# A GLA/SSD/conv-FFN decoder layer: the first four gate pairs of the up projection as plain products of unnormalised h

## The chip, the cores and the metric

The kernel runs on one core of one Trainium2 chip. The metric is the time of one execution in device microseconds. Engines are named as in the profile: PE multiplies matrices, DVE, ACT and POOL work elementwise, SP issues DMAs.

## The reference

One layer on 576 tokens: 512 of one new sequence and 64 of eight running ones (8 each). D_MODEL is 2048, FFN_DIM 5632, all in fp32.

```python
def _layer(x, s_gla, s_ssd, s_conv, s_ffn, p):
    xn = _rmsnorm(x, p['n_mix_pre'])
    mix, g_new, h_new, c_new = _mixer(xn, s_gla, s_ssd, s_conv, p)
    x = x + _rmsnorm(mix, p['n_mix_post'])          # h
    xn = _rmsnorm(x, p['n_ffn_pre'])
    f, f_new = _conv_ffn(xn, s_ffn, p)
    x = x + _rmsnorm(f, p['n_ffn_post'])
    return x, g_new, h_new, c_new, f_new

def _conv_ffn(xn, s_ffn, p):
    u = xn @ p['ffn_w_in']                          # 2048 -> 2 x 5632
    u, buf = _causal_dwconv(u, s_ffn, p['ffn_conv_w'], p['ffn_conv_b'])
    a, b = jnp.split(u, 2, axis=-1)
    return (jax.nn.silu(a) * b) @ p['ffn_w_out'], buf.astype(xn.dtype)
```

## The kernel before

Activations lie transposed: 128 features on the partitions, 576 tokens (T) along the free axis, HALF = 288 of them in a PSUM bank. A vector of 2048 features is KT = 16 k tiles. Each fp32 product is made of three fast ones (type fp32r): both factors are split into a high part, rounded by ACT's copy, and a low part, the rest, subtracted by DVE or POOL; then hi x hi, hi x lo and lo x hi are summed. Weights arrive in units of eight 128x128 blocks (512 KB): SP loads them into one of two `raw` slots, ACT writes w_hi (`weight_hi`, `two_hi`), POOL writes w_lo (`weight_lo`), in a ring of four. SP may refill a raw slot when its low part is done.

In order of time the kernel has the input projection with the GLA and SSD mixers woven in, the output projection (32 half tiles, until some 934 us), the h stage, the up projection with conv and gate, the down projection, and the last norm.

**The h stage.** While the output projection's second half runs, DVE adds its halves to the mix tiles, ACT squares them, and DVE adds the squares to `sqsum`. PE sums that over the partitions with one-column matmuls, ACT and DVE make the reciprocal root of the few columns, and PE spreads it over the partitions into PSUM (`work[:, 2:4]`). Then, tile by tile, DVE multiplies the mix tile by it and by norm_mix_post (semaphore h_m), POOL (tiles 0 to 10, POOL_H) or DVE (11 to 15) adds x: this is h. ACT squares h into one of two sq buffers and stores h to DRAM in pairs; PE's `h_arrives` sums the square of a tile over the partitions with six one-column matmuls and adds three fill-in matmuls (`keep_clock` does so elsewhere). When all 16 are summed, the root is made again, spread by PE and copied to `rstd`.

**The up projection.** It makes 2 x 44 tiles of 128 features: 44 pairs (FT) of a gate tile and its partner. Each pair is computed by Winograd's form of the 2x2 product: the two output tiles by two halves of the k tiles, against two halves of the tokens. Seven products take the place of eight. For each pair of k tiles j (KP = 8), DVE's `form(j)` normalises h (two multiplies) and makes four sums and differences (T1 to T4); with the three plain parts these are seven operands of 288 columns. ACT's `x_highs(j)` copies all 2016 columns, DVE's `x_lows(j)` subtracts 1440 of them and POOL's `x_lows(j)` 576. A unit of weights serves two k pairs: 14 products of three matmuls; DVE forms four sums from it (`weight_sums`), ACT rounds both (`hi_a`, `hi_s`), DVE subtracts both (`weight_lows`). A pair has four units, so 4 x 2 x 7 x 3 = 168 matmuls of 288 columns. Its seven products sit in seven of eight banks; ACT's `p1_copy` reads the first, DVE's `evacuate(g)` the others. The conv's taps (`tap_zero` on ACT, `taps_of` on DVE), `silu` on ACT, `gate_product` on DVE and `g_out` (ACT stores the result) of a pair run during the next one. Each engine's order is the order of its program, written out in loops over w, the weight units.

**The down projection** reads the stored products back, splits them (`g_high`, `g_low`) and multiplies chunk by chunk of k.

## Time and profile before

| | us |
|---|---|
| median of three runs | 2622.26 |
| the runs | 2621.03 to 2623.07 |
| profiled execution, its own time | 2619.91 |
| its span, first to last instruction | 2618.1 |

| busy | us | share of the span |
|---|---|---|
| PE | 2543.0 | 97% |
| DVE | 1616.5 | 62% |
| ACT | 929.8 | 36% |
| POOL | 598.8 | 23% |

Times in the trace count from the start of the span. The page cuts the span into 40 slices; PE's busy share is 90% or more in all but a few: two of them, at some 980 to 1110 us, have 6 and 8 tenths, and the granted clock falls there to 7 and 6 tenths. A busy PE isn't PE at its peak: ends of matmuls are modelled, so the distance from start to start tells the pace. The view by stretches gives each engine's busy time and the granted clock (1.00 is 2.4 GHz, 0.50 is 1.2 GHz). A number in brackets in the timeline is idle time ahead of the instruction, with what ended it.

### The profile page before, as it was taken

The page shows a single profiled execution, that of the slowest core. Times are in us where ns is not written, and L with a number is a line of the kernel's source. Part 1 is how long each engine was busy: PE and PEld are TensorE (multiplying, and loading weights), DVE is VectorE, ACT ScalarE, POOL GpSimd, SP SyncE. Part 2 cuts the span into 40 slices and gives each one's busy share as a digit, 9 for nine tenths or more (in the row PEclk, how much of TensorE's full clock was granted, in tenths as well). Part 3 has the DMA queues.
Part 4 walks back from the last instruction along what each step waited for, and adds up shares of the span by engine and source line. Part 5 has one row for each costly group of instructions (what it writes and reads, how often), then busy time and mean ns, then how long its engine had stood idle before and what let it go on. Part 6 is the DMA issues. An engine that isn't in the chain of part 4 may idle for free.

```text
span 2618.1 us, 49296 instructions
## 1 busy us (share of the span) xinstructions
PE 2543.0 (97%) x20790; PEld 2513.7 (96%) x20790; DVE 1616.5 (62%) x2335; ACT 929.8 (36%) x1288; POOL 598.8 (23%) x285
## 2 busy tenths in 40 slices
PE   8999999999999996899999999999999999999996
PEld 7999999999999996899999999999999999999996
DVE  6544555764336346999999999999999311212105
ACT  6332222533232223544444444444445222112112
POOL 3333223433133321000000000000001334333337
PEclk9999999999999976999999999999999999999998
DMA  4222238523554211333333333333335423242422
GB/s 176 88 83 85 81 123 274 189 74 91 184 187 151 81 63 35 104 111 111 111 104 110 108 107 106 110 111 110 105 110 160 148 88 126 81 134 90 153 84 86
DMA packets 96823, 303.31 MB, mean 116 GB/s; under 512 B 10080, under 2 KB 14816, under 8 KB 95600
## 3 DMA queue, kind: packets, MB, share of 16 engines
q1 hardware_dynamic: 58336, 211.84, 26.4%
...
q14 instruction: 46, 0.38, 0.0%
...
## 4 chain that ended last, share of the span: by engine, by line
PE 88%; DVE 7%; DMA 2%; ACT 1%; POOL 1%; issue 1%; ACTq 0%; POOLq 0%; DVEq 0%; SPq 0%
PE psum_proj L1172 17%; PE psum_proj L1627 9%; PE psum_proj L1628 9%; PE psum_proj L1629 9%; PE psum_work L1627 9%; PE psum_work L1628 9%; PE psum_work L1629 9%; PE psum_proj L1174 8%; PE psum_work L1607 1%; PE psum_work L1612 1%; POOL arena L540 1%; DVE ops_a L2347 1%; DVE arena L2180 1%; DMA out_ssd_s_dram<-arena 1%; DMA raw<-in_weights_dram 1%
## 5 line engine op out<-in xcount | busy, mean ns | idle before, releaser
L483 POOL TENSOR_TENSOR w_lo<-raw,w_hi 128x1024 fp32r<-128x1024 f32 x210 | 521.0, 2482 | 1893.8 <-ACT w_hi L1035 1295.6
L1172 PE MATMUL psum_proj<-x_hi,w_hi 128*128 128x288 f32 (+2 forms) x1696 | 510.6, 301 | 15.0 <-DVE x_lo L1761 13.0
L1172 PE MATMUL psum_proj<-x_lo,w_hi 128*128 128x288 f32 (+2 forms) x1696 | 501.4, 296 | 0.0
L1174 PE MATMUL psum_proj<-x_hi,w_lo 128*128 128x288 f32 (+2 forms) x1696 | 500.8, 295 | 0.0
L1172 PEld LDWEIGHTS psum_proj<-x_hi,w_hi 128*128 128x128 f32 x1696 | 320.6, 189 | 22.2 <-issue 15.5
L1172 PEld LDWEIGHTS psum_proj<-x_lo,w_hi 128*128 128x128 f32 x1696 | 319.8, 189 | 2.6 <-issue 1.9
L1174 PEld LDWEIGHTS psum_proj<-x_hi,w_lo 128*128 128x128 f32 x1696 | 319.5, 188 | 0.0
L550 ACT ACTIVATE w_hi<-raw 128x1024 fp32r<-128x1024 f32 x122 | 128.8, 1056 | 463.1 <-PE psum_proj L1174 402.7
L1627 PE MATMUL psum_proj<-ops_a,w_hi 128*128 128x288 f32 x934 | 276.7, 296 | 6.9 <-DVE ops_a L2290 6.7
L1627 PE MATMUL psum_work<-ops_a,w_hi 128*128 128x288 f32 x916 | 272.4, 297 | 5.4 <-DVE ops_a L2347 5.1
L1628 PE MATMUL psum_proj<-ops_a,w_hi 128*128 128x288 f32 x934 | 276.1, 296 | 0.0
L1629 PE MATMUL psum_proj<-ops_a,w_lo 128*128 128x288 f32 x934 | 276.1, 296 | 0.0
L1629 PE MATMUL psum_work<-ops_a,w_lo 128*128 128x288 f32 x916 | 271.5, 296 | 0.0
L1628 PE MATMUL psum_work<-ops_a,w_hi 128*128 128x288 f32 x916 | 271.4, 296 | 0.0
L1035 ACT ACTIVATE w_hi<-raw 128x1024 fp32r<-128x1024 f32 x88 | 93.3, 1060 | 421.1 <-PE psum_proj L1629 215.4
L907 ACT ACTIVATE w_hi<-tail 128x1024 fp32r<-128x1024 f32 x117 | 124.3, 1063 | 219.1 <-DVE tail L2230 219.1
L1627 PE MATMUL psum_proj<-ops_b,w_hi 128*128 128x288 f32 x608 | 180.4, 297 | 6.7 <-DVE ops_b L2290 6.7
L1627 PEld LDWEIGHTS psum_proj<-ops_a,w_hi 128*128 128x128 f32 x934 | 176.4, 189 | 7.6 <-issue 6.9
L1627 PEld LDWEIGHTS psum_work<-ops_a,w_hi 128*128 128x128 f32 x916 | 173.5, 189 | 7.3 <-DVE ops_a L2347 3.9
L1628 PE MATMUL psum_proj<-ops_b,w_hi 128*128 128x288 f32 x608 | 180.0, 296 | 0.0
L1629 PE MATMUL psum_proj<-ops_b,w_lo 128*128 128x288 f32 x608 | 179.8, 296 | 0.0
L1628 PEld LDWEIGHTS psum_proj<-ops_a,w_hi 128*128 128x128 f32 x934 | 176.3, 189 | 0.0
...
## 6 DMA issues: line engine op xcount, KB each, us to landing
raw<-in_weights_dram SPq DMA_DIRECT2D x386, 512.0 KB, 3.6
...
```

Of the source, the lines that this page charges most:

```text
L483: nc.gpsimd.tensor_tensor(w_lo[:, slot], raw[:, r], w_hi[:, slot].bitcast(F32), ALU.subtract).then_inc(lo_ready, 1)
L540: nc.gpsimd.tensor_tensor(a, a, cut(x_hi[:, kt].bitcast(F32), n), ALU.add).then_inc(added_p, 1)
L550: nc.scalar.activation(w_hi[:, slot], raw[:, r], ACT.Copy).then_inc(hi_ready, 1)
L907: nc.scalar.activation(w_slot(w, 0)[:, 6:14], w_sum, ACT.Copy).then_inc(whs_ready, 1)
L1035: nc.scalar.activation(w_hi[:, (2 + v) % 4], raw[:, v % 2], ACT.Copy).then_inc(hi_ready, 1)
L1172: nc.tensor.matmul(banks[:, n, 0:b - a], w_hi[:, slot, k], (hi, lo)[part][:, a:b], start=first and part == 0, stop=False)
L1174: mm = nc.tensor.matmul(banks[:, n, 0:b - a], w_lo[:, slot, k], hi[:, a:b], start=False, stop=last)
L1607: mm = nc.tensor.matmul(work[0:w, 0, 448 + 3 * n + i:449 + 3 * n + i], cut(sq[kt % 2], n)[:, t:t + w], ones[:, 0:1], start=kt == 0 and n = ...
L1612: nc.tensor.matmul(work[:, 1, 0:P], ones[:], ident[:], start=True, stop=True)
L1627: nc.tensor.matmul(to, w_h, hi, start=first, stop=False)
L1628: nc.tensor.matmul(to, w_h, lo, start=False, stop=False)
L1629: return nc.tensor.matmul(to, w_l, hi, start=False, stop=last)
```

## The change

The first four gate pairs (STD = 4) are no longer computed by seven products but by the eight of the plain form, 2 outputs x 16 k tiles x 2 cuts of the tokens x 3 matmuls, from operands that aren't normalised yet: ACT writes h x norm_ffn_pre as the high part as each h tile comes (`x_std`), DVE the low part (`x_low_std`). The factor 1/rms of a token is applied when DVE reads the banks (`take_std`). So PE can start with the first h tile; in the first pair each k tile's square is summed over the partitions by two matmuls of 288 columns against a full matrix of ones (`sum_tokens`), which leaves the sum on all partitions; ACT's root and DVE's reciprocal then run on all 576 columns. The six one-column matmuls, the fill-in matmuls of a tile, the spreading of the root by PE and the copy of it go.

The operands of the seven products are formed during the plain pairs: DVE normalises h in place behind the first pair, and `form`, `x_highs` and `x_lows` come in pieces as room is freed. The plain operands of the 16 k tiles take the room of the seven-product operands, so pairs 2 to 5 of these wait for the fourth plain pair's progress (`tile_mm`, STD_FREES) and are written out by hand in the programs of ACT and DVE. POOL now adds x for all 16 tiles, splits the weights of the 16 plain units as it does in the projections before, and no longer takes a part of the x low parts. The x rows are reloaded into other room, earlier, right behind the last GLA part. The seven-product form runs over 40 pairs. The last pair takes its units in the order 1, 2, 0, 3, the down projection its banks in another order, and h comes back with its tiles swapped in pairs, all as the layout asks.

The core of the diff:

```diff
+STD = 4
+W_UNIT0 = FFN_UNIT0 + STD * UP_UNITS
+WUNITS = (FT - STD) * UP_UNITS
...
+STD_FREES = (1, 5, 10, 12)
+LAST_UNITS = (1, 2, 0, 3)
...
+        def x_std(kt, low):
+            if kt < 2:
+                return w_third[:, T * (2 * kt + low):T * (2 * kt + low + 1)]
+            slot = 2 * kt - 4 if kt < 6 else 2 * kt + 4 if kt < 12 else 2 * kt - 16
+            return ops_a[:, T * (slot + low):T * (slot + low + 1)]
...
-            for kt in range(POOL_H):
+            weights_lo(at_ynorm + 1, at_h - 1)
+            for j in range(4):
+                if j == 3:
+                    pool.wait_ge(sq_free, KT + 2)
+                weight_lo(4 * at_h - 2 + j, (2 + j) % 4, j % 2)
+            for kt in range(KT):
                 pool.wait_ge(h_m, kt + 1)
-                pool.wait_ge(block_in[kt // 4], 16)
+                pool.wait_ge(block_in[kt // 4], 64 if kt >= 12 else 16)
                 nc.gpsimd.tensor_tensor(h_of(kt), h_of(kt), xres(kt), ALU.add).then_inc(added_p, 1)
-            x_lows(0)
-            x_lows(1)
...
+            weights_lo(at_h, (W_UNIT0 - 2) // 4)
...
+                    two_hi(4 * i + OUT_UNIT0 + 4 + d0, 2 * i + OUT_UNIT0 // 2 + 2 + d0 // 2, 2)
+                    for j in range(4):
+                        act.wait_ge(taken, 4 * i + j + OUT_TILE0 + d0 + 3)
+                        act.wait_ge(sq_free, 4 * i + j + 8 * c + 1)
+                        nc.scalar.activation(sq[j % 2], mix_of(c, i, j).rearrange("p o t -> p (o t)"),
+                                             ACT.Square).then_inc(squared, 1)
+                        if j == 1:
+                            two_hi(4 * i + OUT_UNIT0 + 6 + d0, 2 * i + OUT_UNIT0 // 2 + 3 + d0 // 2, 0)
...
+                act.wait_ge(added_p, kt + 1)
+                nc.scalar.activation(x_std(kt, 0), h_of(kt), ACT.Copy, scale=V("ffn_pre", kt)).then_inc(op_high, 1)
                 if kt >= 2:
                     act.wait_ge(hsq_mm, kt - 1)
                 nc.scalar.activation(sq[kt % 2], h_of(kt), ACT.Square).then_inc(squared, 1)
...
+                if kt == 11:
+                    hi_std(4)
...
             act.wait_ge(hsq_mm, KT)
-            roots_of_columns(work[:, 0, 448:451], work[:, 0, 451:454], mroot)
-            hi_a(1)
-            act.wait_ge(msum_mm, 3)
-            nc.scalar.activation(halves(rstd[:]), work[:, 0:2, 0:HALF], ACT.Copy).then_inc(mroot, 1)
+            root(rstd[:], work[:, 0:2, 0:HALF], 1.0 / D, mroot)
+            hi_std(5)
...
+                a = DIRECT * HALF
+                nc.scalar.activation(x_ops(j, 0)[:, 0:a], h_pair(j)[:, 0:a], ACT.Copy)
+                nc.scalar.activation(x_ops(j, 0)[:, a:], x_sums(j)[:, a:], ACT.Copy).then_inc(op_high, 1)
...
+            hi_std(6)
+            hi_std(7)
+            states_in(0)
+            tap_zero(0, 0)
+            tap_zero(0, 1)
+            new_states(0)
+            silu(0)
+            g_out(0)
+            hi_std(8)
+            hi_std(9)
             x_highs(0)
             x_highs(1)
+            hi_std(10)
+            hi_std(11)
+            states_in(1)
+            tap_zero(1, 0)
+            tap_zero(1, 1)
+            new_states(1)
+            silu(1)
+            g_out(1)
+            hi_std(12)
+            hi_std(13)
+            hi_std(14)
+            hi_std(15)
+            hi_a(0)
+            states_in(2)
+            tap_zero(2, 0)
+            tap_zero(2, 1)
+            hi_s(0)
+            new_states(2)
+            silu(2)
+            g_out(2)
+            x_highs(2)
+            hi_a(1)
             hi_s(1)
-            for w in range(WUNITS):
-                g, u = w // UP_UNITS, w % UP_UNITS
+            x_highs(3)
+            x_highs(4)
+            hi_a(2)
+            x_highs(5)
+            hi_s(2)
+            states_in(3)
+            tap_zero(3, 0)
+            tap_zero(3, 1)
+            act.wait_ge(taken, UP_TAKEN0)
+            act.dma_start(fstate[:, 672:], fconv_in.rearrange("p b c -> p (b c)")[:, 672:]).then_inc(ffn_in, 16)
+            x_highs(6)
+            x_highs(7)
+            hi_a(3)
+            hi_s(3)
+            new_states(3)
+            hi_a(4)
+            hi_s(4)
+            silu(3)
+            g_out(3)
...
+                sum_tokens([sq[kt % 2]], 0, hsq_mm, kt == 0, kt == KT - 1)
+                pe.wait_ge(op_low, kt + 1)
+            def up_std(g):
+                order = LAST_STD if g == STD - 1 else range(KT)
+                steps = [(0, 1, 2, 3)] + [(i,) for i in range(4, KT)] if g == 1 else [(i,) for i in range(KT)]
+                rings = (3, 2) if g % 2 else (1, 0)
+                if g >= 2:
+                    pe.wait_ge(taken, STD_TAKEN0 + 2 * (g - 1))
+                for step in steps:
+                    for j in range(2):
+                        if g == 1 and j and 0 in step:
+                            pe.wait_ge(mroot, 2)
+                        for i in step:
+                            kt = order[i]
+                            half, k = kt // 8, kt % 8
+                            n = 4 * g + 2 * half + j
+                            if g == 0 and j == 0:
+                                h_arrives(kt)
+                            if i % 8 == 0:
+                                pe.wait_ge(lo_ready, FFN_UNIT0 + n + 1)
+                            mm = products((2 + n) % 4, k, rings[j], 256, i == 0, i == KT - 1, x_std(kt, 0), x_std(kt, 1))
+                            if j and i % 8 == 7:
+                                mm.then_inc(units_done, 2)
+                            if j and g == STD - 1 and i in STD_FREES:
+                                mm.then_inc(tile_mm, 1)
+            for g in range(STD):
+                up_std(g)
...
+                    if g == STD:
+                        pe.wait_ge(op_low, X_OPS0 + kp + 1)
...
+                            if g == STD and q in (0, 4):
+                                pe.wait_ge(taken, UP_TAKEN0 - (2 if q == 0 else 0))
...
+            def x_low_std(kt):
+                ve.wait_ge(op_high, kt + 1)
+                stt(x_std(kt, 1), h_of(kt), V("ffn_pre", kt), x_std(kt, 0).bitcast(F32), ALU.mult, ALU.subtract)\
+                    .then_inc(op_low, 1)
...
+                if kt >= 2:
+                    x_low_std(kt - 2)
...
+            ve.wait_ge(mroot, 2)
+            own(nc.vector.reciprocal(rstd[:], rstd[:]))
+            settle()
+            def normalise(j):
+                h = h_pair(j)
+                stt(h[:, 0:T], h[:, 0:T], V("ffn_pre", 2 * j + 1), rstd[:], ALU.mult, ALU.mult)
+                own(stt(h[:, T:2 * T], h[:, T:2 * T], V("ffn_pre", 2 * j), rstd[:], ALU.mult, ALU.mult))
...
+                if 2 <= j < 5:
+                    ve.wait_ge(tile_mm, j)
+                if j == 5:
+                    ve.wait_ge(units_done, W_UNIT0)
+                if j in (1, 6, 7):
+                    ve.wait_ge(op_low, X_OPS0 + j)
...
+                tt_op(x_ops(j, 1)[:, 0:a], h_pair(j)[:, 0:a], x_ops(j, 0)[:, 0:a].bitcast(F32), ALU.subtract)
+                tt_op(x_ops(j, 1)[:, a:], x_sums(j)[:, a:], x_ops(j, 0)[:, a:].bitcast(F32), ALU.subtract)\
...
+            def take_std(g, j):
+                pd, banks = fpad[j], pair_of_banks(((1, 0), (3, 2))[g % 2][j])
...
+                tt_op(pd[:, FC - 1:FC - 1 + SEQ].rearrange("p (n t) -> p n t", n=2), banks[:, :, 0:256],
+                      rstd[:, 0:SEQ].rearrange("p (n t) -> p n t", n=2), ALU.mult)
+                tt_op(sample_cols(pd[:, FC - 1 + SEQ:])[:, :, FC - 1:], sample_cols(banks[:, 1, 256:320]),
+                      sample_cols(rstd[:, SEQ:T]), ALU.mult).then_inc(taken, 1)
...
+            take_std(0, 0)
+            take_std(0, 1)
+            ve.wait_ge(h_st, 128)
+            for j in range(4):
+                normalise(j)
+            taps_of(0, 0)
+            taps_of(0, 1)
+            for j in range(4, KP):
+                normalise(j)
+            gate_product(0)
+            for j in range(2):
+                form(j)
+                x_lows(j)
+            take_std(1, 0)
+            take_std(1, 1)
+            taps_of(1, 0)
+            taps_of(1, 1)
+            gate_product(1)
+            take_std(2, 0)
+            take_std(2, 1)
+            weight_sums(0)
+            taps_of(2, 0)
+            taps_of(2, 1)
+            weight_lows(0)
+            gate_product(2)
+            form(2)
             weight_sums(1)
-            x_lows(0)
-            x_lows(1)
-            for w in range(WUNITS):
-                g, u = w // UP_UNITS, w % UP_UNITS
-                if g == 0 and u < 3:
-                    form(2 * w + 2)
+            x_lows(2)
+            weight_lows(1)
+            form(3)
+            form(4)
+            x_lows(3)
+            x_lows(4)
+            take_std(3, 0)
+            take_std(3, 1)
+            form(5)
+            weight_sums(2)
+            x_lows(5)
+            weight_lows(2)
+            weight_sums(3)
+            form(6)
+            x_lows(6)
+            form(7)
+            x_lows(7)
+            weight_lows(3)
+            weight_sums(4)
+            taps_of(3, 0)
+            taps_of(3, 1)
+            gate_product(3)
```

## Rows read from the trace of the kernel before

**Rows 1.** The page, busy time, share of the span and instructions: PE.
```profile
PE 2543.0 (97%) x20790; PEld 2513.7 (96%) x20790; DVE 1616.5 (62%) x2335; ACT 929.8 (36%) x1288; POOL 598.8 (23%) x285
```
**Rows 2.** Stretches: length, busy us of each engine (instructions), PE clock, DMA share, GB/s.
```profile
942.00:950.00 8.00, 8.00 (x73) 7.85 (x72) 8.00 (x13) 2.73 (x4) 7.82 (x6) 1.00 0.51 174
950.00:970.00 20.00, 20.00 (x106) 19.66 (x105) 10.10 (x11) 4.10 (x6) 8.80 (x6) 0.52 0.27 101
...
1012.00:1027.00 15.00, 7.69 (x44) 7.52 (x45) 14.83 (x19) 4.59 (x4) 3.97 (x3) 0.73 0.12 36
...
1400.00:1800.00 400.00, 400.00 (x3026) 400.00 (x3025) 378.56 (x631) 191.32 (x289) 0.00 (x0) 1.00 0.36 109
```
**Rows 3.** Timeline of ACT (start, duration, what): the copies of a first product.
```profile
1061.72 0.41 ACT L972 ACTIVATE smalls<-psum_proj 128x288 f32<-128x288 f32 x1 [0.56 <-PE psum_proj L1629]
...
1085.17 0.41 ACT L972 ACTIVATE smalls<-psum_work 128x288 f32<-128x288 f32 x1 [0.24 <-PE psum_work L1629]
...
2020.86 0.38 ACT L972 ACTIVATE smalls<-psum_work 128x288 f32<-128x288 f32 x1
```
**Rows 4.** Timeline of PE in the h stage and at the first seven-product matmul.
```profile
944.85 1.34 PE L1607 MATMUL psum_work<-ones,arena 128*128 128x1 f32 x12
...
954.88 2.18 PE L1607 MATMUL psum_work<-ones,arena 128*128 128x1 f32 x12
...
958.43 2.19 PE L1607 MATMUL psum_work<-ones,arena 128*128 128x1 f32 x12
...
1012.57 0.58 PE L1627 MATMUL psum_proj<-ops_a,w_third 128*128 128x288 f32 x1 [6.73 <-DVE ops_a L2290]
```
**Rows 5.** Timeline of PE at the kernel's start: sums of squares among projection matmuls.
```profile
28.23 1.13 PE L1204 MATMUL psum_work<-arena,ones 128*128 128x288 f32 x4
...
32.36 1.13 PE L1204 MATMUL psum_work<-arena,ones 128*128 128x288 f32 x4
```
**Rows 6.** Timeline of DVE: the post-norm multiplies of 16 tiles.
```profile
941.28 11.69 DVE L2256 SCALAR_TENSOR_TENSOR arena<-x_flat,vec,psum_work 128x576 f32<-128x576 f32 x16 [0.25 <-PE psum_work L1596]
```
**Rows 7.** Timeline of POOL: the adds of x, 11 tiles.
```profile
942.18 16.62 POOL L517 TENSOR_TENSOR arena<-arena,x_flat 128x576 f32<-128x576 f32 x11 [30.19 <-DVE arena L2256]
```
**Rows 8.** Timeline of DVE: first and last difference of a form, an x low part.
```profile
1003.15 0.46 DVE L2278 TENSOR_TENSOR x_flat<-x_flat 128x288 f32<-128x288 f32 x1
...
1004.39 0.45 DVE L2283 TENSOR_TENSOR x_flat<-x_flat 128x288 f32<-128x288 f32 x1
...
1024.53 1.65 DVE L2290 TENSOR_TENSOR ops_a<-x_flat,ops_a 128x1440 fp32r<-128x1440 f32 x1
```
**Rows 9.** Timeline of DVE: weight sums, taps, weight low parts, the next sums (first instructions).
```profile
1069.82 0.69 DVE L2226 TENSOR_TENSOR tail<-raw 128x512 f32<-128x512 f32 x1
...
1071.35 0.83 DVE L2332 SCALAR_TENSOR_TENSOR x_flat<-x_flat 128x592 f32<-128x592 f32 x1
...
1072.97 0.95 DVE L2235 TENSOR_TENSOR w_third<-raw,w_third 128x768 fp32r<-128x768 f32 x1
...
1075.16 0.69 DVE L2226 TENSOR_TENSOR tail<-raw 128x512 f32<-128x512 f32 x1
```
**Rows 10.** Timeline of DVE at the kernel's start: a reciprocal of all tokens.
```profile
42.55 3.75 DVE L1775 RECIPROCAL rstd<-rstd 128x576 f32<-128x576 f32 x1 [2.27 <-ACT rstd L562]
```
**Rows 11.** Timeline of DVE: one subtraction beside POOL's weight splits, and alone.
```profile
2016.59 15.70 DVE L2347 TENSOR_TENSOR ops_a<-x_flat,ops_a 128x576 fp32r<-128x576 f32 x11 [2.58 <-ACT ops_a L1028]
...
2057.22 0.75 DVE L2347 TENSOR_TENSOR ops_a<-x_flat,ops_a 128x576 fp32r<-128x576 f32 x1
```
**Rows 12.** Timeline of ACT: the high parts of one k pair's seven operands.
```profile
1004.88 1.88 ACT L965 ACTIVATE ops_a<-x_flat 128x2016 fp32r<-128x2016 f32 x1 [3.34 <-DVE x_flat L2283]
```
**Rows 13.** The page, DMA issues: KB each and median us to landing.
```profile
raw<-in_weights_dram SPq DMA_DIRECT2D x386, 512.0 KB, 3.6
```
**Rows 14.** The page, costliest groups: POOL's splits and ACT's copies of a weight unit.
```profile
L483 POOL TENSOR_TENSOR w_lo<-raw,w_hi 128x1024 fp32r<-128x1024 f32 x210 | 521.0, 2482 | 1893.8 <-ACT w_hi L1035 1295.6
...
L550 ACT ACTIVATE w_hi<-raw 128x1024 fp32r<-128x1024 f32 x122 | 128.8, 1056 | 463.1 <-PE psum_proj L1174 402.7
```

354 lines of the change are left out of this document (152 added, 202 removed).

## The prediction

> **What bounds the kernel now.** I read the page first: PE is busy 97% of the span [rows 1], so a change gains only where PE idles, runs at its lower clock, or is given less to do. The table of stretches names the place. In 1400 to 1800 us PE is busy throughout at clock 1.00, with DVE at 378.56 of 400 us; from 950 to 970 us PE looks busy at clock 0.52 (the stretch up to 1001 is like it), and from 1012 to 1027 it is busy for half of the time (the next two stretches of 15 us are like it) [rows 2]. The timeline of PE tells what it did: up to 997 us it summed squares with one-column matmuls and filled up with matmuls that nobody reads, one h tile in 3.55 us (954.88 to 958.43) [rows 4]. Then it waited for DVE four times, some 7 us each, because the operands of the seven products come in pairs from DVE (the wait of 6.73 before 1012.57 stands for the four). ACT's copy of the first product of each gate pair is a good clock hand: call its start S(g). S(0) = 1061.72, S(1) = 1085.17, S(43) = 2020.86 [rows 3]. From S(1) on a pair takes (2020.86 - 1085.17)/42 = 22.28 us, which is 168 matmuls at 0.1326 us. PE bounds that part, DVE is 5% behind it.
>
> So between the first h tile at 944.85 [rows 4] and S(0) lie 116.9 us for 150 matmuls (19.9 us) of useful work: 97 us are lost. The change lets PE multiply there. Everything up to some 934 us and everything from S(5) on is the same work in the same order (the order of the last pair's units and of the banks in the down projection only rename what is free), so the sum is the shift of S(5). Before, S(5) = 1085.17 + 4 x 22.28 = 1174.3.
>
> **Start.** ACT now makes the high part of the fourth plain unit ahead of the squares of the last two mixer tiles, and this copy waits for the last mixer matmul. It costs one copy of 1.06 us [rows 14], of which I take 0.75 as exposed (at most 1.1, at least 0: the last mixer tile has to be read by DVE first, and that runs beside it). DVE's first weight sum and split leave this place, but PE's fill-in matmuls covered them: nothing. The x tiles are loaded earlier, and nobody waits for them. First h sum on PE: 944.85 + 0.75 = 945.6.
>
> **First plain pair.** 16 k tiles x 2 outputs x 2 halves x 3 = 192 matmuls; at 0.1326 that is 25.5 us. The squares now go through 128x288 fp32 matmuls against ones. The trace has this pattern at its start: 24 projection matmuls with one such sum repeat every 32.36 - 28.23 = 4.13 us [rows 5], so a sum costs 4.13 - 24 x 0.1326 = 0.95 us, 16 of them 15.2. Is PE fed? It needs a tile every 2.54 us. POOL adds 16 tiles instead of 11 at 16.62/11 = 1.51 us [rows 7]; DVE gives 0.73 us to the post-norm [rows 6] and 0.75 to 1.5 us to the low part; ACT gives two passes, each at most as long as DVE's. All are quicker: PE bounds. The pair ends at 945.6 + 40.7 = 986.3. PE has dense work from 945.6 on, while its clock fell only at some 950 us, after 5 us of one-column matmuls [rows 2]; I take the full clock.
>
> The sum of a tile is its four instructions of 288 columns. The Trainium skill, FP8 and Floating Point Precision, lists true FP32 as four passes through the array; by that two matmuls would cost 8 x 0.133 = 1.06 us and the sixteen 17 us. The row, 0.95, is a little cheaper than this estimate, and I use the row.
>
> **Second pair.** It runs 25.5 us, to 1011.8. Its second output needs the bank of the sums and the next weight unit: root, weight copy and POOL split are 0.7 (an estimate from the 0.73 of DVE for as many columns) + 1.06 + 2.48 [rows 14] = 4.2 us against 1.6 + 3.2 us of PE work; covered, up to 0.5 if not. DVE starts at 985.5 with the reciprocal of 576 columns, 3.75 us [rows 10] (the old way inverted a few columns), then takes the first pair out (four multiplies from PSUM, 1.5, as the post-norm's 0.73 for 576 columns [rows 6]), then 4 pairs of normalisation, 8 x 0.74 = 5.9, taps 3.25 [rows 9], the other 8 normalisations 5.9, gate product 0.75. That is 1006.5 if DVE is alone. It isn't: POOL now splits twelve more units, and DVE's subtractions that cost 0.75 us alone took 15.70/11 = 1.43 while four POOL splits ran [rows 11], 1.9 us lost for each. Two splits fall into the normalisations: 1009.9. Behind that gate product ACT stands in g_out, and behind it the copies of units 8 and 9, which PE needs at once for the third pair: they end at 1011.0 and 1012.0, POOL's splits at 1013.5 and 1016.0. PE waits 1.7 and, after one step of 0.8, 1.7 more: 3.4 us (0 if DVE is undisturbed, 7 if each split costs its whole 2.48 and the normalisations queue). I add 1 for matmuls at the lower clock behind it; behind a wait of 6.7 us the trace has a dozen or more of them.
>
> The Trainium skill says this of the two engines (GPSIMD Engine Reference, Key points): GpSimd shares its SBUF interfaces with VectorE, and instructions with two SBUF inputs contend. [rows 11] agree, 1.43 against 0.75. It speaks against leaving the weight splits of the plain units to POOL.
>
> **Third and fourth pair.** Third: to 1011.8 + 3.4 + 1 + 25.5 = 1041.7. In it DVE has 29 us of work at most and reaches its end idle. Fourth: to 1067.2. Its work for DVE can't begin at 1041.7: the two weight buffers are held by units 14 and 15, whose copies wait for the third pair's end. Copy 1.06, split 2.48, DMA 3.6 [rows 13] put the first seven-product unit into place at 1048.8. From there DVE has, in its order: sums 1.53, a wait for ACT's first tap 0.4, taps 3.25, low parts 2.0 to 2.19, gate product 0.75, form 1.65, sums 1.5, wait 0.5, x low parts 2.3, weight low parts 2.1, two forms 3.3, x low parts 2.4 and 2.3: 24 us [rows 8, 9]. (A form is now only its four subtractions, 1003.15 to 1004.84; the x low parts cover 2016 columns where 1440 took 1.65 [rows 8], so 2.3, because POOL's share has gone to DVE.) Only then come the two reads of the fourth pair's banks, 1.5: 1074.3. But PE's fifth product of the fifth pair wants those banks at 1067.2 + 12 x 0.1326 = 1068.8. **First new wait: 5.5 us.**
>
> **Fifth pair.** From 1074.3 PE runs the ten products that are left of unit 0 (4.0, to 1078.3), unit 1 to 1083.9 and unit 2 to 1089.4. Unit 3 needs x pairs 6 and 7 and the fourth split of weights. DVE by then: three forms 5.0, two weight sums 3.0, three x low parts 6.8, two weight low parts 4.1, and between form and low part ACT's copy of 2016 columns, 1.88 [rows 12], exposed twice in full and once by 0.5 because this form, copy, subtract goes pair by pair: 4.4. Sum 23.3: 1097.6. **Second new wait: 8.2 us.** Before, POOL took 576 of the 2016 columns and two forms overlapped the copies.
>
> Then sums 1.5, taps 3.25, gate product 0.75, low parts 2.1: 1105.2, where PE has ended the pair at 1103.2; sums 1.5, and the pair's five bank reads at 0.46 us and a short wait each [rows 8] until PE's seventh product may start: 1109.6. From there to the first product of the last k pair are 132 matmuls, 17.5 us: S(5) = 1127.1. The clock behind the two waits hides under DVE; I add 0.5. 1127.6 against 1174.3 is **46.7 us** less. From here DVE has 1 us per pair in hand and PE's pitch of 22.28 holds.
>
> Check of the sum from the other side: 96 more matmuls (4 x 24) 12.7, sums 15.2, start 0.75, waits 3.4 + 1 + 5.5 + 8.2 + about 3.5 from S(4) to S(5) (4.7 there, less the 1.2 that S(0) to S(1) lost before) make 50.3; 97 less 50.3 is 46.7.
>
> The profiled execution took 2619.91 us for a span of 2618.1; it is 2.35 below the median of the three runs, 2622.26. 2619.9 - 46.7 = 2573.2, and at the median 2575.6: **2576 us**.
>
> **The rivals.**
> - *All waits are covered.* If DVE is little disturbed, the banks free earlier and the last operands come in time, PE alone bounds: 945.6 + 40.7 + 76.5 + 22.3 + 19.9 = 1105.0 for S(5), 69.3 less, **2553 us**. Against it stands DVE's share of 95% in the steady part [rows 2]: it has no room for the eight operand pairs, and the order take after form is fixed. Chance 0.10.
> - *DVE and ACT queue longer.* If each POOL split costs DVE 2.5 us, if a blocked wait of ACT (g_out, the weight copies behind it) repeats at the third and fourth pair, and if the sixth pair's backlog lasts, some 14 us come on top: **2590 us** (2585 to 2600). Chance 0.20.
> - *PE isn't fed in the first pair.* Now POOL's add meets DVE's low parts. From 2.54 us an add on, against 1.51 now, the tiles bound; at 3.0 some 7 us are lost: 2583. That is inside the forecast's spread; it would mean that the squares aren't PE's price but POOL's.
> - *Slower.* The clock stays at 1.2 GHz as it does behind 950 us now [rows 2]. Each us of plain work at that clock costs another one. The plain stage and sums hold 117 us of it; the gain of 46.7 is gone once 47 us of that work run at the lower clock (94 us of time), and if all do the time is 2576 + 117 less the waits it hides (18), about **2675 us**. For it: fp32 sums and short waits break the stream. Against it: at the start of the kernel the same mixture ran at 4.13 us a round, which leaves 0.1326 us for a matmul only at full clock [rows 5]. Chance 0.03.
>
> **How the numbers follow.** Forecast as worked out, 2562 to 2585: 0.66; covered 0.10; longer queues 0.20; slower 0.03; anything between 0.01. The unknown terms are the start (0 to 1.1), the third pair's wait (0 to 7), the two new waits (together 8 to 20) and the clock behind them (0 to 5); low 2557 and high 2590 leave out most of the covered case and half of the longer queues. Within 0.2% is what a measurement of this kernel can't tell from no change, 5.2 us here; faster 0.96, same 0.01, slower 0.03.
>
> **What would show it.** In the profile of the changed kernel: the first h sums some 0.75 us later; the first plain pair 40 to 41 us long with a tile every 2.5 us and clock 1.00; a wait of 2 to 4 us for a POOL split at the start of the third pair; a wait of PE for DVE's bank reads four products into the fifth pair, 5 to 6 us; one of about 8 us for the x low parts ahead of its last unit; the last first-product copy at 1974 instead of 2020.86, and from there to the end nothing moved. The prediction is wrong if PE's stream in the plain stage is broken by the clock, if the waits in the fifth pair are missing, or if DVE's backlog runs on past the seventh pair.

## The result, and the profile after

The changed kernel takes 2575.94 us (median of 4 runs, 2574.82 to 2577.95) against 2622.66 us for the kernel before beside it: ratio 0.9821, interval 0.9804 to 0.9839. The forecast was 2576, range 2557 to 2590. The profiled execution took 2575.91 us for a span of 2574.1, that is 44.0 less than the one of before. The forecast's sum, made against the profiled execution, said 46.7 less; the next section but one comes back to the 2.7 between.

The page after, PE's line, to be held against [rows 1]:

```profile
PE 2509.8 (98%) x20626; PEld 2478.6 (96%) x20626; DVE 1575.5 (61%) x2251; ACT 925.4 (36%) x1288; POOL 636.1 (25%) x298
```

Stretches of the changed kernel (length, busy us and instructions of each engine, PE clock, DMA share, GB/s), which answer [rows 2]:

```profile
945.00:960.00 15.00, 14.99 (x96) 13.54 (x95) 14.49 (x16) 9.87 (x16) 15.00 (x9) 1.00 0.31 119
...
1012.00:1020.00 8.00, 5.18 (x28) 4.90 (x28) 5.76 (x6) 2.11 (x4) 3.85 (x2) 0.79 0.46 133
...
1064.00:1072.00 8.00, 4.69 (x36) 4.46 (x34) 7.48 (x13) 4.58 (x5) 0.00 (x0) 1.00 0.22 66
...
1075.00:1088.00 13.00, 12.91 (x79) 12.91 (x80) 10.49 (x19) 6.34 (x8) 0.00 (x0) 0.79 0.25 71
...
1094.00:1110.00 16.00, 10.15 (x55) 9.69 (x55) 14.80 (x22) 7.11 (x12) 0.00 (x0) 0.79 0.28 85
```

In the h stage PE is busy at clock 1.00 where it had 0.52. Three holes are left: at 1012, from 1068 and from 1093. PE's waits by what ended them (total, times, longest) name them:

```profile
PE psum_work L1698 <- DVE x_flat L2403: 6.4, 1, 6.4
PE psum_proj L1698 <- issue: 6.1, 1, 6.1
PE psum_proj L1698 <- DVE ops_a L2451: 5.0, 3, 2.2
...
PE psum_proj L1232 <- POOL w_lo L511: 2.8, 2, 1.6
...
PE psum_proj L1698 <- DVE x_flat L2413: 1.0, 1, 1.0
PE psum_work L1649 <- DVE tail L2280: 0.7, 1, 0.7
```

L2403 is DVE's read of the fourth pair's banks. "issue" is the wait in front of the fifth pair's last unit: PE goes on at 1098.90, and DVE's last low part for that unit ends at 1098.80:

```profile
1097.58 1.22 DVE L2316 TENSOR_TENSOR w_third<-tail,w_third 128x1024 fp32r<-128x1024 f32 x1
```

L2413 is DVE's first read of the fifth pair's banks, L2280 its sum of squares ahead of the h stage, L2451 the split of gate products between up and down projection, L511 POOL's split of a weight unit. ACT's copies of first products, the time marks of [rows 3], now S(4), S(5) and S(43):

```profile
1105.90 0.39 ACT L986 ACTIVATE smalls<-psum_proj 128x288 f32<-128x288 f32 x1
...
1128.93 0.41 ACT L986 ACTIVATE smalls<-psum_work 128x288 f32<-128x288 f32 x1 [0.19 <-PE psum_work L1700]
...
1975.04 0.39 ACT L986 ACTIVATE smalls<-psum_proj 128x288 f32<-128x288 f32 x1
```

### The profile page after: what moved, and what is told of

Same layout as the page of the kernel before. It is cut to its first block, busy times and chain, and to the rows that moved or that the text cites. A ratio compares the mean times of both kernels' runs of the same rounds, so it can differ in the third digit from the quotient of the medians.

```text
span 2574.1 us, 48954 instructions
## 1 busy us (share of the span) xinstructions
PE 2509.8 (98%) x20626; PEld 2478.6 (96%) x20626; DVE 1575.5 (61%) x2251; ACT 925.4 (36%) x1288; POOL 636.1 (25%) x298
## 4 chain that ended last, share of the span: by engine, by line
PE 54%; DVE 3%; POOL 1%; issue 1%; ACT 0%; DMA 0%; POOLq 0%; DVEq 0%; SPq 0%; ACTq 0%
PE psum_proj L1698 9%; PE psum_proj L1700 9%; PE psum_work L1698 9%; PE psum_work L1700 9%; PE psum_proj L1699 9%; PE psum_work L1699 9%; POOL arena L561 1%; DVE ops_a L2451 1%; POOL arena L552 1%; DMA raw<-in_weights_dram 0%; DVE w_lo L2316 0%; DVE w_lo L2312 0%; DVE ops_a L2383 0%; ACT ops_a L979 0%; DVE tail L2301 0%
## 5 line engine op out<-in xcount | busy, mean ns | idle before, releaser
L511 POOL TENSOR_TENSOR w_lo<-raw,w_hi 128x1024 fp32r<-128x1024 f32 x226 | 561.9, 2488 | 1917.9 <-ACT w_hi L1050 1260.6
L571 ACT ACTIVATE w_hi<-raw 128x1024 fp32r<-128x1024 f32 x138 | 145.3, 1057 | 501.3 <-PE psum_proj L1234 426.8
L1698 PE MATMUL psum_proj<-ops_a,w_hi 128*128 128x288 f32 x890 | 264.4, 297 | 5.0 <-DVE ops_a L2451 5.0
L1700 PE MATMUL psum_proj<-ops_a,w_lo 128*128 128x288 f32 x890 | 263.7, 296 | 0.0
L1699 PE MATMUL psum_proj<-ops_a,w_hi 128*128 128x288 f32 x890 | 263.5, 296 | 0.0
L1700 PE MATMUL psum_work<-ops_a,w_lo 128*128 128x288 f32 x876 | 258.0, 295 | 0.0
L1698 PE MATMUL psum_work<-ops_a,w_hi 128*128 128x288 f32 x876 | 257.9, 294 | 0.0
L1699 PE MATMUL psum_work<-ops_a,w_hi 128*128 128x288 f32 x876 | 257.7, 294 | 0.0
L1050 ACT ACTIVATE w_hi<-raw 128x1024 fp32r<-128x1024 f32 x88 | 93.3, 1060 | 422.8 <-PE psum_work L1700 222.0
L1698 PEld LDWEIGHTS psum_proj<-ops_a,w_hi 128*128 128x128 f32 x890 | 168.7, 190 | 6.5 <-DVE ops_a L2451 3.8
L1698 PE MATMUL psum_proj<-ops_b,w_hi 128*128 128x288 f32 x568 | 168.2, 296 | 1.0 <-DVE x_flat L2413 1.0
L1700 PEld LDWEIGHTS psum_proj<-ops_a,w_lo 128*128 128x128 f32 x890 | 168.7, 190 | 0.0
L1699 PEld LDWEIGHTS psum_proj<-ops_a,w_hi 128*128 128x128 f32 x890 | 168.7, 190 | 0.0
L1700 PE MATMUL psum_proj<-ops_b,w_lo 128*128 128x288 f32 x568 | 167.6, 295 | 0.0
L1699 PE MATMUL psum_proj<-ops_b,w_hi 128*128 128x288 f32 x568 | 167.5, 295 | 0.0
```

The costliest lines, as they stand in the source:

```text
L511: nc.gpsimd.tensor_tensor(w_lo[:, slot], raw[:, r], w_hi[:, slot].bitcast(F32), ALU.subtract).then_inc(lo_ready, 1)
L571: nc.scalar.activation(w_hi[:, slot], raw[:, r], ACT.Copy).then_inc(hi_ready, 1)
L1050: nc.scalar.activation(w_hi[:, (2 + v) % 4], raw[:, v % 2], ACT.Copy).then_inc(hi_ready, 1)
L1698: nc.tensor.matmul(to, w_h, hi, start=first, stop=False)
L1699: nc.tensor.matmul(to, w_h, lo, start=False, stop=False)
L1700: return nc.tensor.matmul(to, w_l, hi, start=False, stop=last)
```

## The experiments

All times are medians, each beside runs of the kernel before on the same chip (2622.2 to 2623.4 us). Up to the first sum of squares of h the changed kernel and its variants (a_) have the same code, and yet it started between 945.6 and 948.1 us in their profiled executions; before and b_ones, alike up to there as well, have 944.9 and 945.6. So S is counted from that start, and the table splits the span in three.

| kernel | first h sum | S(5) after it | S(43) after it | from S(43) to the span's end | median us |
|---|---|---|---|---|---|
| before | 944.9 | 229.2 | 1076.0 | 597.2 | 2622.66 |
| b_ones | 945.6 | 198.2 | 1046.1 | 597.7 | 2591.13 |
| changed | 945.9 | 183.0 | 1029.1 | 599.1 | 2575.94 |
| a_again | 946.5 | 184.4 | 1030.1 | 599.0 | 2577.46 |
| a_half_sums | 946.3 | 179.0 | 1025.1 | 595.7 | 2569.51 |
| a_take_early | 946.2 | 183.2 | 1029.1 | 599.0 | 2576.72 |
| a_pool_lows | 945.6 | 185.8 | 1032.0 | 599.3 | 2578.98 |
| a_fill | 946.1 | 181.0 | 1026.1 | 598.8 | 2571.97 |
| a_taps_early | 946.6 | 182.0 | 1028.2 | 596.3 | 2575.06 |
| a_hi_first | 946.1 | 187.0 | 1033.4 | 599.1 | 2580.65 |
| a_hi2 | 947.5 | 183.8 | 1030.5 | 599.0 | 2577.89 |
| a_ghigh | 946.9 | 184.4 | 1029.4 | 592.8 | 2572.24 |
| a_best2 | 948.1 | 178.6 | 1024.4 | 594.0 | 2568.36 |
| a_best3 | 948.0 | 174.5 | 1019.5 | 595.3 | 2563.62 |

The changed kernel run again shows how far a row may be trusted:

> The changed kernel itself once more, on the chip of the two kernels beside it, as their measure: 2576 us (2574.5 to 2577.5), S(43) 1029 us after the first sum of squares of h.

It came out at 2577.46 us, S(43) at 1030.1. At S(5) the two profiles of one kernel differ by 1.4 us, at S(43) by 1.0. Most of the 1.4 is ACT's, not PE's. Timeline of ACT, first in the changed kernel, then in a_again:

```profile
1128.93 0.41 ACT L986 ACTIVATE smalls<-psum_work 128x288 f32<-128x288 f32 x1 [0.19 <-PE psum_work L1700]
```

```profile
1130.07 0.85 ACT L941 ACTIVATE w_third<-raw 128x768 fp32r<-128x768 f32 x1 [2.44 <-DMA raw<-in_weights_dram]
1130.82 0.39 ACT L986 ACTIVATE smalls<-psum_work 128x288 f32<-128x288 f32 x1
```

In a_again the copy stood behind another one, which waited for its weights. A matmul of PE itself is a better mark. The one called P below comes 24 matmuls ahead of the end of the product that is copied at S(5). Timeline of PE, first in the changed kernel, then in a_again:

```profile
1125.57 0.30 PE L1698 MATMUL psum_work<-ops_b,w_hi 128*128 128x288 f32 x1
```

```profile
1126.22 0.30 PE L1698 MATMUL psum_work<-ops_b,w_hi 128*128 128x288 f32 x1
```

Counted from the first h sum, P is at 179.6 and 179.8 us. So in the table less than 1.5 us proves nothing, while P differs by 0.1 between these two profiles (two are few). By S(43) PE's own stream is 0.6 apart.

**The sums alone.**

```diff
 # kernel before, squares of h
-one-column matmuls of sq against ones, per token tile; three filling matmuls
+sum_tokens([sq[kt % 2]], 0, hsq_mm, kt == 0, kt == KT - 1)
 # behind the last tile
-matmuls that spread the root; 12 filling matmuls
+pe.wait_ge(h_m, KT); 24 filling matmuls
 # rstd
-roots of columns, reciprocals of columns, spread by PE, copy by ACT
+root(rstd[:], work[:, 0:2, 0:HALF], 1.0 / D, mroot); nc.vector.reciprocal(rstd[:], rstd[:])
```

> The kernel before with one part of the change alone: the squares of h go through matmuls against ones (sum on every partition), root on 576 columns, reciprocal of 576 columns on DVE (3.75 us); no spread back over the partitions, no filling matmuls between the tiles; the first four gate pairs stay in seven products as before. My theory (both parts of the change bring a share, and the sums the larger one): the 3.55 us per h tile fall to what POOL's add allows, 1.5 to 1.9 us, 16 x 1.8 = 28 us, and the chain of root, spread and reciprocals (some 5 us) becomes root and one reciprocal (some 4.5): about 28 us less than before, 2594 us, S(5) at some 1146. Then the plain products bring the remaining 19. Rival 1 (the plain products carry the change): the tile pace is set by something that stays, ACT's squares or the clock of 1.2 GHz, a tile still takes 3 us or more and at most 9 us go. Rival 2 (PE at the lower clock bounds the tile): four passes of 288 columns at half clock take 1.9 us and not 0.95, the pace is 1.9 to 2.0 us, 25 us less.

Measured: 2591.13 us, ratio 0.9886 (0.9870 to 0.9901), 31 less by the medians and 29.9 less at S(43). Timeline of PE:

```profile
956.56 1.24 PE L1202 MATMUL psum_work<-arena,ones 128*128 128x288 f32 x4 [0.64 <-ACT arena L950]
958.44 1.24 PE L1202 MATMUL psum_work<-arena,ones 128*128 128x288 f32 x4 [0.64 <-ACT arena L950]
...
982.27 0.58 PE L1613 MATMUL psum_proj<-ops_a,w_third 128*128 128x288 f32 x1 [10.24 <-DVE ops_a L2277]
```

A tile takes 1.88 us in these rows and 1.3 us over the sixteen (945.61 to 966.50), where it took 3.55 [rows 4] and 1.5 to 1.9 were expected. The waits that the view has there, three of 0.64, are for ACT's squares. Rival 1 is out, and rival 2 as well: the clock in the stretches from 945 to 976 us was 1.00. So, counted in this order, two thirds of the gain come from the sums (with the shorter chain behind them) and one third, 17 us at S(43), from multiplying during them. PE still waits 10.2 us for the first pair of operands, and that stretch is what the plain products fill.

**What a sum costs PE.**

```diff
-sum_tokens([sq[kt % 2]], 0, hsq_mm, kt == 0, kt == KT - 1)
+if kt % 2 == 0: sum_tokens([sq[0]], 0, hsq_mm, kt == 0, False)
+else: two matmuls of 8 columns against ones into the same banks
```

> The changed kernel, with PE summing the squares of every second h tile only; for the others it adds 8 columns of each half (so that it still waits for the squares and reports them), and the mean is doubled. Half of the squares are left out of the norm; ACT, POOL and DVE do all their work. Theory (PE bounds the first plain pair, and a sum costs it 0.95 us): the pair takes 40.7 - 8 x 0.95 + 8 x 0.1 = 33.9 us instead of 40.7, and as everything behind it hangs on PE, S(5) and the end come 6 to 7 us earlier, 2569.5 us. Rival (the tiles come from POOL, ACT and DVE no faster than every 2.5 us, the sums ride in PE's slack): pair still 40 us or more, time the same within 1 us.

Measured: 2569.51 us, the number that was expected, and for half of the reason only. Timeline of PE:

```profile
960.20 1.13 PE L1264 MATMUL psum_work<-tail,ones 128*128 128x288 f32 x4
...
962.76 0.51 PE L1669 MATMUL psum_work<-tail,ones 128*128 128x8 f32 x4
...
964.79 1.13 PE L1264 MATMUL psum_work<-tail,ones 128*128 128x288 f32 x4
```

Two tiles take 4.59 us (960.20 to 964.79) instead of 5.08. Of these 24 x 0.1326 = 3.18 us are the products of two tiles, so both sums cost 1.41. With 0.95 for the full one the sum of 8 columns costs 0.46, not 0.1. Eight of those saved 4 us, S(5) and S(43) came 4.0 earlier. This shows PE as what bounds the first pair (tiles every 2.30 us were fed as well as tiles every 2.54), and it shows the expectation's price for 8 columns wrong. The remaining 3.4 us came from the other end: from S(43) on the span is 595.7 instead of 599.1. Between up and down projection PE waited for DVE twice and not three times:

```profile
PE psum_proj L1704 <- DVE ops_a L2457: 3.3, 2, 2.2
```

and the last stretch with dense work (30 us, from 540 us behind S(43)) ran at full clock, where the changed kernel lost some. First row the changed kernel, second the one with half of the sums:

```profile
2515.00:2545.00 30.00, 28.66 (x207) 28.24 (x206) 12.21 (x28) 13.99 (x29) 20.93 (x23) 0.94 0.03 11
```

```profile
2511.40:2541.40 30.00, 28.56 (x215) 27.91 (x214) 15.32 (x36) 14.96 (x33) 23.82 (x26) 1.00 0.01 1
```

Had only the time been looked at, a wrong price would have passed as confirmed.

**POOL as a helper.**

```diff
+POOL: x_ops(j, 1)[:, 1440:2016] = x_sums(j)[:, 1440:] - x_ops(j, 0)[:, 1440:]   # j = 5, 6, 7
-DVE:  x_ops(j, 1)[:, 864:2016]
+DVE:  x_ops(j, 1)[:, 864:1440]
```

> The changed kernel, with POOL forming 576 of the 2016 columns of the x low parts of the h pairs 5, 6 and 7 again, as it did for all pairs before the change (DVE forms 1440). Theory (the two engines contend for SBUF, so POOL gives nothing): a DVE operation of 1440 columns takes 1.65 us alone; while POOL's part runs it takes some 2.3 to 2.8, as long as DVE takes for all 2016 alone; POOL's own part takes 1.3 us or more and can end after DVE's. The second wait of PE in the fifth pair stays at 6 us, time the same or up to 2 us more. Rival (POOL is a free helper): three times 0.65 us less on DVE's chain, the second wait 2 us shorter, time 2 us less.

Measured: 2578.98 us, 1.5 and 3.0 more than the two measurements of the changed kernel, which is hardly more than their own distance. But P comes 2.7 us later, and the trace shows why. DVE's second subtraction has half of the columns and takes longer than the whole one had. Timeline of DVE in the changed kernel, then of DVE in this one, then of POOL in this one:

```profile
1079.66 1.35 DVE L2383 TENSOR_TENSOR ops_a<-x_flat,ops_a 128x1152 fp32r<-128x1152 f32 x1
```

```profile
1079.39 1.99 DVE L2393 TENSOR_TENSOR ops_a<-x_flat,ops_a 128x576 fp32r<-128x576 f32 x1
```

```profile
1078.46 2.30 POOL L547 TENSOR_TENSOR ops_a<-x_flat,ops_a 128x576 fp32r<-128x576 f32 x1 [30.83 <-ACT ops_a L984]
```

POOL's subtraction runs from 1078.46 to 1080.76. DVE's, begun at 1079.39, ends at 1081.38, 0.62 us behind POOL's end, and 576 columns alone take it 0.75 [rows 11]. So DVE stood until POOL had finished. The Trainium skill says just that (SBUF — State Buffer, SBUF: two separate sides): the shared pair of ports is an exclusive lock that the first of the two holds for its whole instruction. The trace agrees, three times in this kernel (1.99, 1.99 and 1.97 us). Three times 0.64 us more than 1.35 make 1.9 of the 2.7 us; the rest wasn't traced.

**One chain or two waits.**

```diff
+take_std(3, 0); take_std(3, 1)
 x_lows(3)
 x_lows(4)
-take_std(3, 0); take_std(3, 1)
```

> The changed kernel, with DVE's two reads of the fourth pair's banks (1.5 us in all) put ahead of the x low parts of pairs 3 and 4 (4.7 us) instead of behind them. Theory (both waits of PE are for one and the same chain of DVE, which works without a pause from 1049 to the last low parts of unit 3): PE's first wait shrinks from 6.4 to 1.7 us or less, PE then stands longer in front of the fifth pair's last unit (from 6 to 8 or more us), S(5) and the time stay within 0.7 us, of which a gain could come from the matmuls at the lower clock behind the wait, that are now fewer. Rival (the bank wait is a price of its own): the time falls by what the wait loses, 4.7 us.

Measured: 2576.72 us, S(5) at 183.2. PE's waits:

```profile
PE psum_proj L1698 <- DVE w_third L2316: 8.4, 1, 8.4
...
PE psum_work L1698 <- DVE x_flat L2403: 1.3, 1, 1.3
```

The first wait went from 6.4 to 1.3, the second from 6.1 to 8.4, and between them, at 1082.7, a new one of 2.7 came up: 12.4 in all, where it was 12.5. P is 0.7 us earlier, S(43) and the time are the same. The two waits are one debt, DVE's, and it can be paid in either place.

**Filling DVE's holes.** Twice the changed kernel lets DVE stand between a form and its low parts:

```profile
1088.38 1.06 DVE L2382 TENSOR_TENSOR ops_b<-arena,ops_b 128x864 fp32r<-128x864 f32 x1 [2.05 <-ACT ops_b L979]
...
1094.47 1.06 DVE L2382 TENSOR_TENSOR ops_b<-arena,ops_b 128x864 fp32r<-128x864 f32 x1 [2.04 <-ACT ops_b L979]
```

```diff
-weight_sums(3)
 form(6)
+weight_sums(3)
 x_lows(6)
 form(7)
+taps_of(3, 0)
 x_lows(7)
 weight_lows(3)
 weight_sums(4)
-taps_of(3, 0)
```

> The changed kernel, with DVE's two idle stretches of 2.05 us in the fifth pair (it forms the sums of an h pair and then stands until ACT has copied them) filled: the weight sums of unit 3 go behind the sums of pair 6, the first tap of gate pair 3 behind the sums of pair 7. Theory (one DVE chain from 1049 us on sets S(5); what it idles in is lost one for one): the low parts of unit 3 end 1.5 to 2 us earlier, the taps behind them are 1.6 us shorter, S(5) comes 3 us earlier, and the time falls by 3 us (2 to 3.5), where the clock at the two later places with waits (between up and down projection, and at the end) may add or take 1 to 2. Rival (weights, their transfers or ACT bound the fifth pair, not DVE): S(5) moves by less than 1 us.

Measured: 2571.97 us, 4.0 less than the changed kernel. S(5) is 1.9 earlier, but its copy stood in ACT's queue again; P is 3.2 earlier and S(43) 3.0. The wait in front of the last unit is 4.4 instead of 6.1. The theory holds.

```diff
 # DVE; on ACT hi_a(0) and hi_s(0) go behind silu(2)
-weight_sums(0)
 taps_of(2, 0); taps_of(2, 1)
-weight_lows(0)
 gate_product(2)
+weight_sums(0); weight_lows(0)
```

> The changed kernel, with taps and gate product of gate pair 2 put ahead of the first weight sums of the seven-product part on DVE (and their ACT steps ahead of the first copy of weight sums), into the 5.8 us in which DVE stands for the weights' transfer. Theory (same DVE chain): of these some 4.4 us of DVE work up to 4 move into the idle stretch, S(5) comes 2.6 us earlier (0 if the two POOL splits that run there slow the taps, 4.4 at most), and the first wait of PE in the fifth pair shrinks from 6.4 by the same. Rival (the chain hangs on the next transfer of weights, which would then be waited for instead): less than 1 us.

Measured: 2575.06 us, which the time alone can't tell from the changed kernel; P is 1.0 earlier. DVE's chain came 1.9 us earlier (its low part of pair 7 at 1093.20 with a start that lay 0.6 later, against 1094.47), and of PE's waits the first fell from 6.4 to 4.5 while the second rose from 6.1 to 6.9. Of the 4.4 us that were moved, 2 went to one collision, this tap beside POOL's split, 0.83 alone:

```profile
1046.85 2.85 DVE L2438 SCALAR_TENSOR_TENSOR x_flat<-x_flat 128x592 f32<-128x592 f32 x1
```

Neither theory holds in full: some of the idle time reached PE, less than half of the 2.6 us expected, and POOL's split took a part of what was missing.

**ACT's queue order, and the wait that travels.**

```diff
-g_out(0)
 hi_std(8); hi_std(9)
+g_out(0)
```

> The changed kernel, with ACT's weight copies of the units 8 and 9 ahead of its write of the first gate product (which waits for DVE's gate product at 1009.5). Theory (the waits of 1.6 and 1.2 us at the start of the third pair come from this queue order): the copies are made as soon as PE frees the places, POOL splits 3 us earlier, both waits go, and with them the matmuls at the lower clock behind them: PE reaches the fourth pair's end 3 to 3.6 us earlier, S(5) and the time the same. Rival (POOL's earlier splits slow DVE's normalisation and taps, and the operands are late instead): half of it or less.

Measured: 2580.65 us, 4.0 later at S(5) and at P: slower than the changed kernel. The waits at the third pair's start did go (in 1012 to 1020 PE was busy for all of the 8 us, where it had 5.18). Timeline of POOL, of DVE, and of PE at its next wait:

```profile
1004.69 5.75 POOL L511 TENSOR_TENSOR w_lo<-raw,w_hi 128x1024 fp32r<-128x1024 f32 x2 [7.60 <-ACT w_hi L571]
```

```profile
1005.23 2.95 DVE L2353 SCALAR_TENSOR_TENSOR arena<-arena,vec,rstd 128x576 f32<-128x576 f32 x1
1008.11 2.95 DVE L2352 SCALAR_TENSOR_TENSOR arena<-arena,vec,rstd 128x576 f32<-128x576 f32 x1
```

```profile
1028.32 0.80 PE L1232 MATMUL psum_proj<-ops_a,w_hi 128*128 128x256 f32 x2 [3.53 <-POOL w_lo L511]
```

Two normalisations took 2.95 us instead of 0.81. ACT then stood behind DVE's sums, with the copies of the units 10 and 11 behind that, and the price came out bigger half a pair later: waits of 3.5 and 1.1 us, and behind them the lower clock. The stretch in the changed kernel, then in this one:

```profile
1028.00:1044.00 16.00, 16.00 (x125) 16.00 (x124) 5.88 (x9) 4.76 (x6) 6.87 (x4) 1.00 0.46 145
```

```profile
1028.00:1044.00 16.00, 14.63 (x83) 14.23 (x84) 6.13 (x6) 3.47 (x7) 7.87 (x4) 0.72 0.50 151
```

Neither theory had it in this size; the rival had the direction.

```diff
 hi_std(8); hi_std(9)
 g_out(0)
+hi_std(10); hi_std(11)
 x_highs(0); x_highs(1)
-hi_std(10); hi_std(11)
```

> The changed kernel, with ACT's weight copies of the units 8 to 11 pulled ahead: 8 and 9 ahead of the write of the first gate product, 10 and 11 right behind it and ahead of the two copies of h pair sums. With only 8 and 9 pulled ahead the waits at the third pair's start went, but POOL's two splits took 4.3 us from DVE, ACT stood behind DVE's sums, and the copies of 10 and 11 queued behind that gave PE a wait of 3.5 us, worse than before. Theory (it is ACT's queue order that turns DVE's delay into a wait of PE): with 10 and 11 out of that queue PE has no wait in the third pair, DVE's delay is lost in its idle stretch of 9.5 us behind it, S(5) and the time come 3 to 4 us earlier than in the changed kernel. Rival (the price of POOL's splits reaches PE whichever way, as DVE's own chain is late): S(5) as in the changed kernel or later, time no less.

Measured: 2577.89 us, nothing won against 2577.46 beside it; the rival's forecast holds. The third pair ran without a wait, and the same wait stood at the start of the fourth, 1.33 and 1.21 us, for the units 12 and 13, which were queued behind gate product 1. The last run of the study moved these too (below), and only then did the gain come.

**Gate products ahead of POOL's splits.**

```diff
-hi_down(0)
+act.wait_ge(units_done, DOWN_UNIT0 - 2)
 g_load(2)
 for q in range(7):
     g_high(q)
+hi_down(0)
```

> The changed kernel, with nothing changed up to the last gate pair; there ACT loads and splits the first seven gate products ahead of the weights of the first down unit, instead of behind them. In the kernel with half of the sums the three waits of PE between up and down projection were 3.3 us instead of 5.0, and DVE's eleven subtractions there took 13.5 instead of 15.7 us, beside one split of POOL less. Theory A (contention: each POOL split of 2.4 to 3 us costs DVE some 2.2 us, and DVE's subtractions are what PE waits for): with seven of the eleven done before POOL's splits start, the waits shrink from 5.0 to 1 us or less, some 1 to 2 us of lower clock go with them, the time falls by 4 to 6 us. Theory B (that difference was only a matter of the clock's phase, and the gate products' transfers bound): waits stay at 4 to 5 us, time within 1.5 us.

Measured: 2572.24 us, 3.7 and 5.2 less than the two measurements of the changed kernel. In the profile it is 592.8 us from S(43) to the end instead of 599.1, but this execution lay 1.5 below its median, and the two kernels below with the same edit have 594.0 and 595.3. Timeline of DVE, in the changed kernel and in this one:

```profile
1970.77 15.70 DVE L2451 TENSOR_TENSOR ops_a<-x_flat,ops_a 128x576 fp32r<-128x576 f32 x11 [2.86 <-ACT ops_a L1043]
```

```profile
1971.03 4.77 DVE L2452 TENSOR_TENSOR ops_a<-x_flat,ops_a 128x576 fp32r<-128x576 f32 x7 [1.62 <-ACT ops_a L1043]
...
1977.85 5.02 DVE L2452 TENSOR_TENSOR ops_a<-x_flat,ops_a 128x576 fp32r<-128x576 f32 x4 [2.05 <-ACT ops_a L1043]
```

Seven subtractions before POOL starts take 0.68 us each, four beside it 1.26. The three waits of 5.0 us for DVE are gone. Two waits for POOL's splits, 1.3 us at 1978 and 1.7 on a later unit, took their place, and the 15 us from 1976 ran 99 matmuls at clock 1.00 instead of 47 at 0.68. Theory A holds for DVE's waits and for the time; it did not foresee the 3.0 us of waits for POOL.

**All together.** The moves of a_fill, a_taps_early, a_hi2 and a_ghigh in one kernel:

> All that helped, together: DVE's idle stretches in the fifth pair filled (3.0 us earlier at S(43), counted from the first sum of squares), taps of gate pair 2 into the wait for weights (0.9), ACT's copies of the units 8 to 11 pulled ahead (3 to 4), gate products split ahead of the first down weights (6.3 behind S(43)). Theory (the places lie one behind the other, PE waits in each): the gains add, 13 us less than the changed kernel, 2563 us; the clock at the waits may take or give 2. Rival (they share one limit, above all POOL's splits and DVE): 8 us or less.

Measured: 2568.36 us, 9.1 less than the changed kernel beside it. That is about the sum of what the four gave alone (3.0, 0.9, 0 and 6.3 in the table make 10.2; 4.7 and 5.1 are found), with a_hi2's expected share missing. Then:

```diff
 x_highs(0); x_highs(1)
+hi_std(12); hi_std(13)
 states_in(1)
 ...
 g_out(1)
-hi_std(12); hi_std(13)
```

> The kernel with all of the moves together, and ACT's weight copies of the units 12 and 13 ahead of the steps of gate pair 1 as well, instead of behind its write. In the two kernels with the copies of 8 to 11 pulled ahead the third pair ran without a wait, but PE then stood 1.4 and 1.2 us at the start of the fourth for the units 12 and 13, whose copies stood behind DVE's taps and gate product 1, with a lower clock behind it; nothing was won. Theory (ACT's queue order): this was the last such place; both waits go, DVE's disturbed subtractions fall into its idle 2.8 us, S(43) comes 3 to 4 us earlier than with all together (1024.4 us after the first sum of squares), the time falls from 2568.4 to some 2565. Rival (three times the same wait at another place: POOL's splits cost DVE more than it has spare up to the fifth pair): the wait turns up in the fifth pair, time 2568 or more.

Measured: 2563.62 us, ratio to before 0.9777 (0.9762 to 0.9792), S(43) at 1019.5 and P at 170.1, 4.9 and 5.1 earlier than without this edit. That is the fastest kernel of the study, 12 to 14 us below the changed one. The weight copies moved alone, without the other edits, weren't run. Its stretches from 1030 us (PE busy throughout, where a_hi2 had its waits, and DVE at 21.44 of 24):

```profile
1030.00:1040.00 10.00, 10.00 (x79) 10.00 (x78) 8.54 (x11) 3.50 (x9) 5.76 (x2) 1.00 0.38 113
1040.00:1064.00 24.00, 24.00 (x185) 24.00 (x184) 21.44 (x34) 10.82 (x17) 4.75 (x2) 1.00 0.34 107
```

In the fifth pair waits of 4.9 and 4.3 us are left, and behind S(43) two for POOL's splits, 1.4 and 2.7; what would remove them wasn't tried.

## Why the prediction was right, step by step

- *Start.* Said 945.6, measured 945.94. PE's wait of 0.7 for DVE's tail is in every changed kernel and neither in before nor in b_ones, so the term is real. The start itself can't confirm it: it moves by 2.5 us between executions, and b_ones, without the wait, has 945.6 too.
- *First pair.* Said a tile every 2.54 us at full clock. PE's sums start at 981.63 and 984.17, 2.54 apart, and the clock is 1.00. The rival in which POOL doesn't feed PE is out: with half of the sums left out the tiles came every 2.30. The price of 0.95 for a sum held here (2.54 less 12 x 0.1326), and it isn't proportional to the columns: 8 of them still cost 0.46. The Trainium skill (FP8 and Floating Point Precision) lists true FP32 as four passes, and the estimate made from that ahead of the result, 1.06, took all of it as proportional; the row of 0.46 speaks against that step.
- *Second pair, third pair's start.* Said the gate product ends at 1009.9, measured 1009.5; waits said 1.7 + 1.7, measured 1.63 + 1.19. The way there was partly luck. I had charged two collisions at 1.9 us, which by my own terms makes 1010.3, not 1009.9. One took 2.15 (2.96 for 0.81, at 994.61); the other fell on the reciprocal and the PSUM reads and cost DVE some 0.3; and DVE had started 0.6 later than said.
- *Fourth pair.* Third pair's end said 1041.7, DVE's read of it starts at 1041.97; first seven-product weights said 1048.8, measured 1049.34.
- *First new wait.* Said 5.5, measured 6.40: DVE's bank reads end at 1074.96 instead of 1074.3, the weights' 0.5 us carried on.
- *Second new wait.* Said 8.2, measured 6.11. Low parts of unit 3 end at 1098.8 instead of 1097.6, and PE came later than said: behind the first wait 79 matmuls fill 13 us that hold 98 at full clock, 2.5 us. I had the clock's cost hidden under DVE, which a_take_early bears out, since wait and clock together left S(5) where it was.
- *S(5).* Said 46.7 less, measured 45.1 (1174.07 to 1128.93, the former read after the result); at S(43) 45.8 [rows 3]. By 1127.6, the forecast's own S(5), that is 1.3 late, and DVE's chain was 1.2 late already at 1098.8.
- *From there to the end.* Here a step failed: "from there to the end nothing moved". The waits between the projections are the same three of 5.0 in all, yet this part is 1.9 us longer, 599.1 against 597.2. Before had:

```profile
PE psum_work L1627 <- DVE ops_a L2347: 5.1, 3, 2.2
```

```profile
2560.90:2590.90 30.00, 28.58 (x215) 27.92 (x214) 13.88 (x33) 14.85 (x32) 22.50 (x24) 1.00 0.01 3
```

The rows place 1.1 us of the 1.9 in this last dense stretch (207 matmuls at clock 0.94 in the changed kernel, 215 at 1.00 as far behind its S(43) before). Another 0.4 stands around the three waits (270 matmuls in the 45 us behind S(43), 273 before); 0.4 isn't placed. a_half_sums and a_taps_early have 595.7 and 596.3, with two waits of 3.3 us for DVE where the changed kernel has three of 5.0; yet a_taps_early too has 0.94 in the last dense stretch. What sets off the lower clock near the end stays open.
- *The number.* 44.0 less by the profiled executions and 46.7 by the medians: the profiled execution of before lies 2.7 below the median of its runs, that of the changed kernel at its median. That 2576 was hit to 0.1 is partly this.

The rivals: *all waits covered* fell with the waits of 6.4 and 6.1; a_best3 reaches 9.6 of its 23 us up to S(43) (1029.1 to 1019.5), with other queue orders. *Longer queues* didn't happen here, but a_hi_first is that very mechanism, made by one line. *PE isn't fed in the first pair* fell with a_half_sums. *Slower* fell with the first stretch shown: from 945 to 960 us, with dense products around the fp32 sums, the clock was 1.00.
